# Seven block products of a feed-forward layer in another order: the last product of a group behind the first of the next, and the weight sums S2 and S1 exchanged

## The reference, cut to what matters

```python
u = jax.nn.relu(rms_norm(h, norm_mlp_g) @ mlp_w1)      # "mlp": 1024 -> 4096 -> 1024
h = h + (u * u) @ mlp_w2

def swiglu(h, w1, w3, w2):                             # "ffn1" and "ffn2": 1024 -> 2816 -> 1024
    return (jax.nn.silu(h @ w1) * (h @ w3)) @ w2
x = x + 0.5 * swiglu(rmsnorm(x, ffn1_norm), ffn1_w1, ffn1_w3, ffn1_w2)
```

## Time and profile before

| | |
|---|---|
| median of 3 runs | 2152.3 us (2151.95 to 2152.45) |
| the profiled execution's own time | 2152.66 us |
| its span | 2150.8 us |
| PE busy | 2123.4 us, 99% |
| PEld busy | 1818.9 us, 85% |
| DVE busy | 1373.3 us, 64% |
| ACT busy | 1031.7 us, 48% |
| seven phases of block products, in sum | 452.2 us |
| granted TensorE clock | 1.0 of full speed in all slices |

### The profile page before, as it was taken

The page is one execution under the profiler, slowest core; times in us unless marked ns, Lnnn a source line. Parts: engine busy times, 40 slices in busy tenths (PEclk is TensorE's granted clock), DMA queues, the critical chain, the costliest instruction groups (busy, mean ns, idle before and its releaser), DMA issues.

```text
span 2150.8 us, 32530 instructions
## 1 busy us (share of the span) xinstructions
PE 2123.4 (99%) x13100; PEld 1818.9 (85%) x13100; DVE 1373.3 (64%) x2281; ACT 1031.7 (48%) x1738; POOL 0.2 (0%) x4
## 2 busy tenths in 40 slices
PE   9999999999999999999999999999999999999999
PEld 7888988888988988898988878887777888899997
DVE  4664663467664767775866677746776356686674
ACT  6654545443433533452543465546666234354344
POOL 0000000000000000000000000000000000000000
PEclk9999999999999999999999999999999999999999
DMA  5121522123233132423322622321111223242421
GB/s 188 60 79 60 191 94 69 41 97 118 79 118 117 61 98 84 133 79 119 117 66 89 200 80 84 99 84 50 32 44 40 79 98 98 92 138 67 136 67 72
DMA packets 190920, 199.74 MB, mean 93 GB/s; under 512 B 8481, under 2 KB 185778, under 8 KB 190258
## 3 DMA queue, kind: packets, MB, share of 16 engines
q1 hardware_dynamic: 190770, 197.66, 29.0%
HBM read 188.73 MB, written 2.10 MB: 89 GB/s over the span
## 4 chain that ended last, share of the span: by engine, by line
PE 84%; DVE 7%; issue 4%; ACT 3%; DMA 1%; SPq 0%; DVEq 0%; ACTq 0%
PE lin L712 19%; PE lin L714 19%; PE lin L713 19%; PE turned L813 3%; PE score L908 3%; PE mix L1256 3%; PE mix L1258 2%; PE mix L1257 2%; PE mix L922 2%; DVE wl L2466 1%; PE score L1256 1%; PE score L1258 1%; PE score L1257 1%; DVE raw L2989 1%; ACT wh L2020 1%
## 5 line engine op out<-in xcount | busy, mean ns | idle before, releaser
L712 PE MATMUL lin<-xh,wh 128*128 128x512 f32 (+1 forms) x1032 | 407.7, 395 | 1.7 <-DVE wl L2461 1.2
L714 PE MATMUL lin<-xh,wl 128*128 128x512 f32 (+1 forms) x1032 | 394.9, 383 | 0.0
L713 PE MATMUL lin<-xl,wh 128*128 128x512 f32 (+1 forms) x1032 | 393.7, 382 | 0.0
L712 PE MATMUL lin<-ah,wh 128*128 128x512 f32 (+1 forms) x788 | 309.1, 392 | 2.9 <-DVE al L2466 2.1
L714 PE MATMUL lin<-ah,wl 128*128 128x512 f32 (+1 forms) x788 | 305.9, 388 | 0.0
L713 PE MATMUL lin<-al,wh 128*128 128x512 f32 (+1 forms) x788 | 305.9, 388 | 0.0
L2455 DVE TENSOR_TENSOR wl<-raw,wh 128x2048 fp32r<-128x2048 f32 x85 | 194.8, 2292 | 123.6 <-ACT wh L1560 123.6
L712 PEld LDWEIGHTS lin<-xh,wh 128*128 128x128 f32 x1032 | 194.2, 188 | 45.8 <-issue 9.6
L714 PEld LDWEIGHTS lin<-xh,wl 128*128 128x128 f32 x1032 | 194.0, 188 | 39.0
L713 PEld LDWEIGHTS lin<-xl,wh 128*128 128x128 f32 x1032 | 194.5, 188 | 34.7 <-issue 1.0
L1560 ACT ACTIVATE wh<-raw 128x2048 fp32r<-128x2048 f32 x85 | 162.0, 1906 | 115.2 <-PE lin L714 108.2
(11 more groups left out here) (446 smaller groups left out, 4279.2 us busy)
## 6 DMA issues: line engine op xcount, KB each, us to landing
raw<-in_w_in_dram SPq DMA_DIRECT2D x38, 1024.0 KB, 5.3
raw<-in_ffn_w_dram SPq DMA_DIRECT2D x28, 1024.0 KB, 5.3
raw<-in_mlp_w_dram SPq DMA_DIRECT2D x20, 1024.0 KB, 5.2
raw<-in_ffn_w_dram SPq DMA_DIRECT2D x32, 512.0 KB, 4.7
raw<-in_xattn_wkv_dram SPq DMA_DIRECT2D x8, 1024.0 KB, 5.4
raw<-in_w_out_dram SPq DMA_DIRECT2D x8, 1024.0 KB, 5.2
xl_f<-in_ffn_w_dram SPq DMA_DIRECT2D x16, 512.0 KB, 5.7
al_f<-in_ffn_w_dram SPq DMA_DIRECT2D x16, 512.0 KB, 5.4
```

What stands on the lines that cost most here:

```text
L712: nc.tensor.matmul(o, w[0], x[0], start=first, stop=False)
L713: nc.tensor.matmul(o, w[0], x[1], start=False, stop=False)
L714: return nc.tensor.matmul(o, w[1], x[0], start=False, stop=last)
```

## The change

Five things change. In phases PE takes the products in the order of `TURN`: A11 of the next group comes ahead of S4 of this one. The block numbers of S1 and S2 are exchanged, so S2 is converted ahead of S1 on ACT and on DVE. In `mlp_phase` and `ffn_phase` S1 of a group and `kept(g, 0)` now stand ahead of the previous group's `finish`, where S2 stood. Phases of two groups start with another set of ring slots. The first panel after a phase takes k 0 to 3 for both column halves, and then k 4 to 7.

```diff
-A11, A12, A22, S3, S1, S2, S4 = range(7)
+A11, A12, A22, S3, S2, S1, S4 = range(7)
+def in_turn(groups):
+
+    order = []
+    for i in range(groups):
+        order += [(i, n) for n in range(6)]
+        if i:
+            order[-6:-5] = [(i, 0), (i - 1, 6)]
+    return order + [(groups - 1, 6)]
...
+def done_count(g, n):
+
+    key, i = PHASE_OF[g]
+    return 7 * PHASES[key][0] + TURN[key].index((i, n)) + 1
...
-    first_ = ([own_, 4, own_ + 1, 5] if n_ == 2 else [4, own_, 5, own_ + 1]) + [other_, other_ + 1]
+    first_ = ([4, own_, own_ + 1, 5] if n_ == 2 else [4, own_, 5, own_ + 1]) + [other_, other_ + 1]
...
-            i_, place_ = divmod(b_ - RING, 7)
+            i_, place_ = TURN[key_][b_ - RING]
...
-                for j in range(panels):
-                    panel_t(p + j, (p + j) % 2, Y, each=made if j == 0 else None)
+                s = p % 2
+                pe.wait_ge(conv_done, p + 1)
+                for k0 in (0, HT):
+                    for c in range(2):
+                        if k0 == 0:
+                            begin(p, c)
+                        cols = slice(c * PART, (c + 1) * PART)
+                        for k in range(k0, k0 + HT):
+                            if c == 0:
+                                made(k)
+                            mm = product(pl[c][:, :], (wh[:, s, k, cols], wl[:, s, k, cols]), (Y[0][:, k, :], Y[1][:, k, :]), k == 0, k == KT - 1)
+                        if k0:
+                            mm.then_inc(lin_done, 1)
+                for j in range(1, panels):
+                    panel_t(p + j, (p + j) % 2, Y)
...
                 for g in range(g0, g0 + n):
                     more = g + 1 < g0 + n
+                    block_high(g, S1)
+                    kept(g, 0, (ml_e, 2 * MLP_G + gate_count(g, -1)))
                     if g > g0:
                         finish(g - 1)
-                    block_high(g, S2)
-                    if g > g0:
                         high(g - 1, RIGHT, E_ur, gate_count(g, 0))
-                    kept(g, 0, (ml_e, 2 * MLP_G + gate_count(g, -1)))
                     block_high(g, S4)
...
-                        block_high(g + 1, S1)
+                        block_high(g + 1, S2)
...
                 for g in range(g0, g0 + n):
                     more = g + 1 < g0 + n
+                    block_low(g, S1)
+                    sum_4(g)
                     if g > g0:
                         finish(g - 1)
-                    block_low(g, S2)
-                    sum_4(g)
-                    if g > g0:
                         low_part(g - 1, RIGHT, E_ur, made_count(g, 0))
                     block_low(g, S4)
...
-                        block_low(g + 1, S1)
+                        block_low(g + 1, S2)
```

More of the change, by code:

```diff
@@ L118 @@
 B11, B21, B22, T1, T2, T3, T4 = range(7)
-A11, A12, A22, S3, S1, S2, S4 = range(7)
+A11, A12, A22, S3, S2, S1, S4 = range(7)
 PRODUCTS = [(A11, B11, 0), (A12, B21, 2), (S2, T2, 0), (S3, T3, 1), (S1, T1, 0), (A22, T4, 1), (S4, B22, 0)]
 PLACE = {a_: n_ for n_, (a_, _, _) in enumerate(PRODUCTS)}
+def in_turn(groups):
[5 more added lines that the diff above has]
+    return order + [(groups - 1, 6)]
+TURN = {key_: in_turn(n_) for key_, (_, n_, _) in PHASES.items()}
+def done_count(g, n):
+    key, i = PHASE_OF[g]
+    return 7 * PHASES[key][0] + TURN[key].index((i, n)) + 1
 RING = 6
@@ L171 @@
 SLOT, SLOT_DONE = {}, {}
-for g0_, n_, p_ in PHASES.values():
+for key_, (g0_, n_, p_) in PHASES.items():
     own_, other_ = 2 * (p_ % 2), 2 * (1 - p_ % 2)
-    first_ = ([own_, 4, own_ + 1, 5] if n_ == 2 else [4, own_, 5, own_ + 1]) + [other_, other_ + 1]
+    first_ = ([4, own_, own_ + 1, 5] if n_ == 2 else [4, own_, 5, own_ + 1]) + [other_, other_ + 1]
     for b_ in range(7 * n_):
@@ L183 @@
             after_ = p_ + (SLOT[g0_, b_] // 2 + p_) % 2
-            SLOT_DONE[after_] = max(SLOT_DONE.get(after_, 0), 7 * g0_ + b_ // 7 * 7 + PLACE[b_ % 7] + 1)
+            SLOT_DONE[after_] = max(SLOT_DONE.get(after_, 0), done_count(g0_ + b_ // 7, PLACE[b_ % 7]))
 SPREADS = {"mix": 0, "xattn": 1, "mlp": 1, "ffn1": 1, "mix2": 1, "ffn2": 2, "final": 2}
@@ L1231, in _, with groups @@
                 panel_t(P0["xo"] + j, (P0["xo"] + j) % 2, Y)
-            def group(g):
-                (net, r), i = PHASE_OF[g]
-                for n, (a, b, at) in enumerate(PRODUCTS):
+            def groups(key):
+                g0 = PHASES[key][0]
+                for i, n in TURN[key]:
+                    g = g0 + i
+                    a, b, at = PRODUCTS[n]
                     o = banks(g)[at].rearrange("p (f n) -> p f n", f=2)
@@ L1263, in phase @@
                 g0, n, p = PHASES[name, r]
-                for g in range(g0, g0 + n):
-                    group(g)
+                groups((name, r))
                 def made(k):
@@ L2022, in kept @@
             def kept(g, n, *free):
-                act.wait_ge(st_q, 7 * g + (1, 3, 4)[n])
+                act.wait_ge(st_q, done_count(g, (0, 2, 3)[n]))
                 for done, count in free:
@@ L2029, in first_blocks @@
             def first_blocks(g):
-                for a in (A11, A12, A22, S3, S1):
+                for a in (A11, A12, A22, S3, S2):
                     block_high(g, a)
@@ L2052, in finish @@
                     k = 4 * (g - g0)
-                    relu(g, E_tr, banks(g)[0].rearrange("p (a n) -> p a n", a=2), [(st_q, 7 * g + 7), (ml_lo, made_count(g, 0))])
+                    relu(g, E_tr, banks(g)[0].rearrange("p (a n) -> p a n", a=2), [(st_q, done_count(g, 6)), (ml_lo, made_count(g, 0))])
                     high(g, k + 2, LEFT, E_ul, (ml_e, 2 * g + 2))
@@ L2058, in mlp_phase @@
                     k, more = 4 * (g - g0), g + 1 < g0 + n
+                    block_high(g, S1)
+                    kept(g, 0, (ml_lo, made_count(g, -3)))
                     if g > g0:
                         finish(g - 1)
-                    block_high(g, S2)
-                    if g > g0:
                         high(g - 1, k - 4, RIGHT, E_tr, (ml_u, made_count(g, 0)))
-                    kept(g, 0, (ml_lo, made_count(g, -3)))
                     block_high(g, S4)
@@ L2096, in finish @@
                 def finish(g):
-                    act.wait_ge(st_q, 7 * g + 7)
+                    act.wait_ge(st_q, done_count(g, 6))
                     act.wait_ge(ml_e, 2 * MLP_G + gate_count(g, 0))
@@ L3018, in made_11 @@
             def made_11(g):
-                dve.wait_ge(st_q, 7 * g + 2)
+                dve.wait_ge(st_q, done_count(g, 1))
                 dve.wait_ge(st_e, 3 * g + 1)
@@ L3024, in made_22 @@
             def made_22(g):
-                dve.wait_ge(st_q, 7 * g + 5)
+                dve.wait_ge(st_q, done_count(g, 4))
                 dve.wait_ge(st_e, 3 * g + 3)
@@ L3030, in made_21 @@
             def made_21(g):
-                dve.wait_ge(st_q, 7 * g + 6)
+                dve.wait_ge(st_q, done_count(g, 5))
                 dve.wait_ge(st_e, 3 * g + 2)
@@ L3047, in later @@
                     sum_2(g)
-                return early, later, lambda: block_low(g, S1)
+                return early, later, lambda: block_low(g, S2)
             def mlp_phase(r):
```

## The result

The changed kernel takes 2156.73 us (median of 12 runs, 2156.31 to 2157.61) beside 2153.01 us for the kernel before (12 runs, 2151.95 to 2153.54): a ratio of 1.0019, 95% interval 1.001 to 1.0027. It is 3.7 us slower where 3.2 us less was forecast, and lies above the range of 2145.6 to 2151.6. The profiled execution has 2156.62 us against the 2149.5 of the sum: 7.1 us too much.

The account below looks back on a forecast made before the run. PE, busy 99% of the span, was taken as the bound, with only its gaps to win. Gaps of 12.8 instead of 13.3 us and panels -2.3 and -0.4 gave -3.2 us: 2149.1 us, range 2145.6 to 2151.6.

Parts of the forecast that it names:

- the sum: Whole kernel: block-product gaps 12.8 us instead of 13.3, panels -2.3 and -0.4, change -3.2 us, giving 2149.5 on the profiled execution.
- Ring slots, loads: Conversions into ring slots wait only for products long done, and loads come about 1 us later; both cost nothing.
- The wait moves from S4 to S1, ended by ACT: Middle ffn groups: S4's 0.53 us gap goes; S1 waits 0.77 with restart for ACT's `kept`, rounds 20.7 us.
- S2 ahead of S1: First group of ffn1 and ffn2: S2's low part comes directly behind its high part, winning 0.25 us in each.
- The carried list of the round: Middle ffn group: DVE and ACT steps from one `kept(g, 1)` to the next, 20.7 us against PE's 19.95.
- The panel: First panel behind each phase, k 0 to 3 first: 2.3 us off behind mlp, some 0.1 at each four ffn phases.
- The gaps simply go: Rival: `kept(g, 1)` in time everywhere, 13.3 + 2.7 us less, 2136.3 us; chance 0.07.
- The round is longer: Rival: every free DVE hand-over costs the waited price, 1.1 us a round, 12 us over eleven rounds, 2161; chance 0.05.

Follow-up runs that it names:

- the slots experiment: Changed kernel with the four-group phases' first slots 4, 5, own, own + 1 instead of 4, own, 5, own + 1; 2149.52 us, ratio 0.9985.
- both cures: Changed kernel with S1 made ahead of S2 again and ACT's kept(g, 1) put ahead of the Silu or Relu; 2137.36 us, ratio 0.9931 to the kernel before.

## Why the prediction was wrong

- *"Ring slots, loads. The slots change only what a conversion waits for, and these products are long done … Both cost nothing."* This is the step that failed. Which product each conversion waits for was not worked out for the phases whose list of slots had stayed the same. The product was the 27th of 28, done 2.8 us ahead of the panel, and the conversion takes 1.91 + 2.29 us. With restarts it costs 7.3 us in the four phases; taking it away brings 7.2 us and the time to 2149.5, against 2149.1 forecast. No rival covered it: each was a variant of the round, none a wait elsewhere.
- *The wait moves from S4 to S1, ended by ACT.* Right. S1's starts in the four-group phases stand 20.68 us apart (20.7 forecast). The gaps with their restarts make 11.0 + 19 x 0.08 = 12.5 us (12.8 forecast).
- *S2 ahead of S1.* The gap at S2 in the first group of ffn1 and ffn2 shrinks, as forecast: over all ten traces it is 0.64 to 1.02 us with S1 first and 0.24 to 0.53 with S2 first. The spread within each is as large as the 0.25 us of the forecast, so the size is not confirmed. But only the place where it wins was priced. The carried list of the round held "sum_2 +1.13, high S2 +1.26, its low +1.08", and the question of what the list would be with S1 there was never put. This hand-over made the round longer than PE's 19.95 us.
- *The panel.* Right: 2.6 us for 2.7, and in the traces 0.8 a mlp phase.
- *The gaps simply go, 2136.3 us, 0.07.* It did not happen here, and its time is nearly that of the kernel with S4's move and S1 made first (2138.1). The limit was neither engine's work: DVE is busy 16.2 of 20.7 us in a round of the slots experiment, as this row of its table by stretch says in its third pair:

```profile
1064.30:1084.99 20.69, 20.18 (x168) 20.00 (x169) 16.19 (x17) 9.77 (x14) 0.00 (x0) 1.00 0.13 44
```

- *The round is longer, by every free hand-over on DVE at the waited price.* It is not: forecast and measured round agree to 0.02 us. The prediction took its rule from the Trainium skill ("VectorE: DVE Perf Modes", section "The DRAIN you can't avoid") without the exception that the same section makes: "A next op that is not held starts earlier". The traces fit the exception: in the last DVE rows above, operations of 1.22 us that wait for nothing start 1.13 and 1.14 us apart. A wait does cost something here, though: two sums in 2.48 us start 1.26 apart.

The mlp phases had the same order with fitting slots and gained what was forecast, so the direction "slower" comes wholly from the slots of the other four phases.

## What to carry to other kernels

When an order changes, work out anew every count that is derived from it, for the phases too whose own tables stay untouched: a buffer lent out is given back by whichever use falls last in the new order. If a wait moves to two engines that hand work to each other, write the ring of hand-overs down and look at each link for a block that could be taken instead while the other engine works; the block that is needed first isn't always the one to make first. Two halves of a change should be costed apart, as one may pay for the other.

## What the runs showed of the hardware

Block products run at one of three rates, with a granted clock of 1.00 (the level of 2.4 GHz) and PE busy throughout in all. In the kernel with S4's move and S1 made first, 21 products in a row (from A11 of the second group to A22 of the last) took 59.14 us in ffn1's first phase, 60.48 in ffn2's first, and 59.80 in ffn1's second: 2.816, 2.880 and 2.848 us a product. The table by stretch:

```profile
901.35:960.49 59.14, 59.14 (x507) 59.14 (x506) 48.22 (x51) 31.00 (x39) 0.00 (x0) 1.00 0.23 72
1896.67:1957.15 60.48, 60.48 (x507) 60.48 (x505) 48.06 (x51) 31.03 (x39) 0.00 (x0) 1.00 0.22 71
1023.97:1083.77 59.80, 59.80 (x506) 59.80 (x505) 48.09 (x51) 31.03 (x39) 0.00 (x0) 1.00 0.23 71
```

The two first phases have a gap of 0.7 and 0.9 us ahead of S2, and go on at the fast rate behind the one and at the slow rate behind the other; the phase without a gap has the middle rate. In the kernel with both cures it is ffn2's phase that is fast and ffn1's that is slow. In all ten traces every phase starts at the middle rate, and every stretch of two products or more between two gaps holds one of the three within 0.002 us. A rate holds until the next gap. Over the 26 products behind such a gap the difference is 0.8 us either way, as much as the gap itself, and that is a good part of what the versions with few gaps differ by. What chooses the rate stays open; no run was made for it.

The three rates also show that no product of PE is in the round of 20.68 us. In the changed kernel and in the slots experiment S1 starts stay 20.68 to 20.70 us apart in the four-group phases, whatever the rate; only the gap ahead of S1 changes, 0.89 to 0.90 us behind products at the fast rate, 0.66 to 0.67 at the middle and 0.44 to 0.45 at the slow one, 0.22 us a step, which is seven products of 0.032. In the kernel before the chain to S4 begins at PE's own S3, two products ahead of it, for which `kept(g, 2)` waits (1049.05 in the earlier trace rows). There the gap hardly changes and the round does: 20.46 us with 0.45 of gap at the middle rate, 20.30 with 0.51 at the fast one.
